# Fox attention in a two-block kernel: probabilities scaled before the value product, two heads in the column halves, head norm by channels

## The chip, the cores and the metric

One core of a Trainium2 chip. The metric is the device time in microseconds of one execution; the median of three runs is given. Engines: TensorE (PE in the profile, PEld for its weight loads), VectorE (DVE), ScalarE (ACT), GpSimd (POOL) and SyncE (SP), which issues the weight DMAs.

## The reference

Two transformer-like blocks for 512 tokens of width 1024, batch 1. The first mixes three heads' families (fox attention, an mLSTM, an HGRN2), projects by `w_out` and adds a convolved gated feed-forward; the second has a differential attention and an MLA attention. The part that is changed is the fox attention with 8 heads of 64, and the norm of its output by head:

```
s = einsum('bhqd,bhkd->bhqk', qi, k) * scale + ci[..., None] - c[:, :, None, :]
p = softmax(where(kpos <= qpos, s, -inf))
oa = einsum('bhqk,bhkd->bhqd', p, v)
ya = rms over each head's 64 channels of oa, times out_g
x = x + concatenate([ya, yb, yc]) @ w_out      # and so on
```

## The kernel before

The whole kernel is one static program. Python builds a list of stages (`order`); every engine walks the same list and issues its own share of each stage, in that order, with semaphores between the engines. So the list fixes the order of work on each engine, and what an engine does late holds back all that stands behind it in its list.

Large products are done as three fp32r products of high and low parts (L1033 to L1035: w_hi by act_hi, w_hi by act_lo, w_lo by act_hi), with activations of 512 tokens moving. Weights arrive by DMA in `w_raw` (two buffers), ScalarE rounds them to `w_hi` (stage `w_hi`), VectorE makes `w_lo` as the difference (stage `w_lo`; in the fox attention the pieces placed by "lo" are halves of 1,024 columns). Each output of 128 channels by 512 tokens is a tile; tiles take turns in two PSUM banks, `ring0` and `ring1`, in the order in which they are first opened. `open_bank` waits until the tile two places earlier has been drained. `tile_done` is one counter for all tiles, and who needs tile n waits until it is n + 1.

The fox attention (`attention("fox", ...)`, L586 and L635) runs over 32 units u, one head h of one query block qb of 128 queries, block by block, 8 heads each. k = qb + 1 key blocks are computed. Its stages are:

- `fox_s`, for two units at once, at even steps: on TensorE scores of two heads in the two row halves (L1254) plus a decay term (L1257), into bank 0 and 1; on VectorE mask and negated row maximum (L1922, with a read of the accumulator); on ScalarE exp with the row sum, into one of four buffers `Pf`.
- `fox_t`, two steps late: TensorE transposes the unit's `Pf` block by block (L1267), VectorE copies the result into `PTs` (L2270).
- `fox_v`, three steps late: TensorE multiplies with `PTs` stationary and 64 columns of the values `av` moving (L1282), into bank 4 or 5, where a query block's eight heads lie side by side, tokens on the partitions.
- After the eighth head: `ya_n` (reciprocal of the row sums, multiply L2278, square on ScalarE), `ya_v` (sum by head L2281, Ln, Exp), `ya_s` (multiply L2286), `ya` (four transposes on TensorE into a ring bank L1290, times `out_g` into `yt` L2292, high part on ScalarE), `ya_l` (low part). They stand 4, 5, 6, 7 and 8 steps behind the block's last head.

Between these, `fill_at` lists other work by step: first the last value tiles and `yb`, then for steps 5 to 37 the tiles `wo_b` 0 to 7 (L1350 to L1352: six matmuls per listed half), each drained by a VectorE add into `xT` (L2308); `w_later` puts the `w_hi` of the two `wo_a` weight chunks at steps 17 and 32, and `lo` halves of `w_lo` at 18, 20, 33 and 34. Then `wo_a` uses all of `ya`. The last entries of `fill_at` are:

```
32: [("w_later", WO_A + 1)], 33: [("lo", 2)], 34: [("wo_b", 6, 2), ("lo", 2)], 35: [("wo_b", 6, 4)],
36: wo_b(6) + [("wo_b", 7, 2), ("wo_b", 7, 4)], 37: wo_b(7), 39: [("hold_lo", False)]
```

Here ("wo_b", j, 2) and ("wo_b", j, 4) are the two halves of tile j on TensorE, and `wo_b(j)` its drain. The MLA attention of the second block (stages `mla_s`, `mla_r`, `mla_t`, `mla_v`) already scales its probabilities by rows on ScalarE after a reciprocal for two heads, and has values stationary.

Two other products in the program use column halves: `hg_win` (L1120, both halves of bank 0) and `hg_in` (L1168, two banks). The norm of q and k uses a product by the constant `blk` (ones within each 64 channels): L1187.

Of the kernel before, what the change touches and what calls it, by code (L numbers as in the profile page):

```python
# [24 lines left out]
P = 128  # L25
# [74 lines left out]
def two_blocks(nc, xt_d, w_in_d, b_in_d, w_gate_d, w_out_d, w_up_d, w_down_d, pos_d, w_in2_d, lam_d, w_uq_d, w_ukv_d,  # L100
               w_pd_d, w_pm_d, w_out2_d, g_fin_d, par_d, con_d, out_d):
    ctx = ExitStack()
    with ctx:
# [6 lines left out]
        def sem(name):  # L110
# [37 lines left out]
        fox_s_mm, fox_m, fox_e, fox_t_mm, fox_pt, fox_v_mm, fox_o_free = (  # L148
            sem(n) for n in ("fox_s_mm", "fox_m", "fox_e", "fox_t_mm", "fox_pt", "fox_v_mm", "fox_o_free"))

        ya_sq, ya_var, ya_rs, ya_n, ya_hi, ys_hi, y_lo = (sem(n) for n in ("ya_sq", "ya_var", "ya_rs", "ya_n", "ya_hi", "ys_hi", "y_lo"))
# [87 lines left out]
        on = sb("on", [P, AH, HD], F32, M + 60)  # L239
        sqA = sb("sqA", [P, AH, HD], F32, M + 62)  # L240
# [135 lines left out]
        def stage(*s):  # L376
            order.append(s)
# [208 lines left out]
        def attention(name, heads, norm, fill_at):  # L586

            n = NB * heads
            for u in range(n + 8):
# [8 lines left out]
                if name == "mla":  # L598
# [4 lines left out]
                    if u % 2 == 0 and u < n:  # L603
                        stage("mla_r", u)
                else:
# [5 lines left out]
                steps = {"ya": ("ya_n", "ya_v", "ya_s", "ya", "ya_l"), "yd": ("yd_n", "yd_s", "yd", "yd_l"), "ym": ("ym", "ym_l")}[norm]  # L611
                for late, kind in enumerate(steps, 4 if name == "fox" else 3):
# [406 lines left out]
        def _(pe):  # L1019
# [57 lines left out]
            for s in order:  # L1077
# [180 lines left out]
                elif kind == "fox_t":  # L1258
                    u = s[1]
                    qb, h = fox[u]  # L1260
                    pe.wait_ge(fox_e, u + 1)
# [7 lines left out]
                elif kind == "fox_v":  # L1269
                    u = s[1]  # L1270
                    qb, h = fox[u]
                    pe.wait_ge(fox_pt, u + 1)
# [8 lines left out]
                    for b in range(qb + 1):  # L1281
                        mm = pe.matmul(bank[4 + qb % 2][:, HD * h:HD * h + HD], PTs[u % 2][:, b * P:b * P + P],  # L1282
                                       av[:, b, HD * h:HD * h + HD], start=(b == 0), stop=(b == qb))
                    mm.then_inc(fox_v_mm, 1)
                elif kind == "ya":
                    qb = s[1]
                    out = open_bank(("ya", qb))
                    pe.wait_ge(ya_n, qb + 1)
                    for j in range(4):
                        mm = pe.transpose(out[:, j * P:j * P + P], on[:, 2 * j:2 * j + 2, :], ident)  # L1290
                    mm.then_inc(tile_done, 1)
# [264 lines left out]
        def _(act):  # L1556
# [23 lines left out]
            for s in order:  # L1580
# [134 lines left out]
                elif kind == "ya_n":  # L1715
                    qb = s[1]
                    act.wait_ge(fox_o_free, qb + 1)
                    A(sqA[:], on[:], ACT.Square).then_inc(ya_sq, 1)
                elif kind == "ya_v":
                    qb = s[1]  # L1720
                    act.wait_ge(ya_var, qb + 1)
                    A(msA, msA, ACT.Ln).then_inc(act_step, 1)
                    act.wait_ge(act_step, step())
# [186 lines left out]
        def _(dve):  # L1910
# [21 lines left out]
            for s in order:  # L1932
# [330 lines left out]
                elif kind == "fox_t":  # L2263
# [4 lines left out]
                    if u >= 2:  # L2268
                        dve.wait_ge(fox_v_mm, u - 1)
# [383 lines left out]
```

## Time and profile before

| | us |
|---|---|
| three runs | 1091.23, 1091.55, 1091.55 (median 1091.55) |
| profiled execution: time | 1091.19 |
| profiled execution: span of the core | 1089.4 |
| TensorE busy | 1076.6 (99%) |
| VectorE busy | 711.6 (65%) |
| ScalarE busy | 429.7 (39%) |
| mean granted clock of TensorE | 0.999 of full speed |

The span runs from the first to the last instruction of the profiled execution. The fox attention lies between 201 us (first scores) and 287 us (first `wo_a` matmul). An f32 matmul call is two instructions in the records (L1254: 64 records for 32 calls); a transpose and a bf16 call are one. In the timeline a matmul's own duration includes its flow through the array, so the pace is read from one start to the next, as the chain does.

### The profile page before, as it was taken

What the parts mean: (1) busy time and instruction counts of PE and PEld (TensorE: products, weight loads), DVE (VectorE), ACT (ScalarE), POOL (GpSimd) and SP (SyncE); (2) the same over time, 40 slices, a digit from 0 to 9 for tenths busy, and PEclk for the clock granted to TensorE, in tenths of its full rate; (3) what the DMA queues carried; (4) which work ended last, traced back from release to release, by engine and by line L of the source; (5) the groups of instructions that cost most, each with busy time, mean ns of one, the idle gap of its engine ahead of it and who ended that gap; (6) DMA issues with size and microseconds to landing.
All of it is one profiled execution on the core that took longest, in us unless ns stands there. A gap on an engine that the chain in (4) does not pass through costs nothing.

```text
span 1089.4 us, 13605 instructions
## 1 busy us (share of the span) xinstructions
PE 1076.6 (99%) x5395; PEld 866.6 (80%) x5395; DVE 711.6 (65%) x1142; ACT 429.7 (39%) x679; POOL 0.2 (0%) x4
## 2 busy tenths in 40 slices
PE   9999999999999999999999999999999999999998
PEld 6877877877878888888888888887776776888886
DVE  6897877867768888754478745655568445464441
ACT  6612555334352323222222234654257545323232
POOL 0000000000000000000000000000000000000000
PEclk9999999999999999999999999999999999999999
DMA  8432121131213233233422234333120321133312
GB/s 255 122 116 79 39 78 42 50 144 39 72 46 126 86 107 105 60 87 97 148 85 75 61 97 155 79 115 116 44 78 14 104 78 39 39 116 116 99 37 78
DMA packets 100239, 95.94 MB, mean 88 GB/s; under 512 B 5952, under 2 KB 91088, under 8 KB 100176
## 3 DMA queue, kind: packets, MB, share of 16 engines
q1 hardware_dynamic: 100000, 95.05, 27.8%
q8 instruction: 43, 0.70, 0.3%
q14 instruction: 20, 0.16, 0.0%
q10 hardware_dynamic: 176, 0.02, 0.0%
HBM read 92.95 MB, written 2.10 MB: 87 GB/s over the span
## 4 chain that ended last, share of the span: by engine, by line
PE 93%; DVE 3%; ACT 2%; issue 1%; DMA 0%; SPq 0%; DVEq 0%; ACTq 0%
PE ring L1033 23%; PE ring L1035 22%; PE ring L1034 22%; PE bank L1033 3%; PE bank L1035 3%; PE bank L1034 3%; PE bank L1491 1%; PE bank L1282 1%; PE bank L1254 1%; PE bank L1187 1%; PE bank L1267 1%; PE bank L1120 1%; PE bank L1460 1%; PE ring L1350 1%; PE bank L1514 1%
## 5 line engine op out<-in xcount | busy, mean ns | idle before, releaser
L1033 PE MATMUL ring<-act_hi,w_hi 128*128 128x512 f32 (+1 forms) x816 | 323.7, 397 | 0.8 <-DVE xT L2313 0.5
L1035 PE MATMUL ring<-act_hi,w_lo 128*128 128x512 f32 (+1 forms) x816 | 316.8, 388 | 0.0
L1034 PE MATMUL ring<-act_lo,w_hi 128*128 128x512 f32 (+1 forms) x816 | 316.6, 388 | 0.0
L1578 ACT ACTIVATE w_hi<-w_raw 128x2048 fp32r<-128x2048 f32 (+4 forms) x97 | 160.8, 1659 | 245.0 <-PE ring L1035 202.6
L1929 DVE TENSOR_TENSOR w_lo<-w_raw,w_hi 128x2048 fp32r<-128x2048 f32 (+5 forms) x102 | 191.4, 1879 | 3.3 <-ACT w_hi L1578 3.0
L1033 PEld LDWEIGHTS ring<-act_hi,w_hi 128*128 128x128 f32 x816 | 153.4, 188 | 37.2 <-issue 3.9
L1034 PEld LDWEIGHTS ring<-act_lo,w_hi 128*128 128x128 f32 x816 | 153.4, 188 | 31.7 <-issue 1.9
L1035 PEld LDWEIGHTS ring<-act_hi,w_lo 128*128 128x128 f32 x816 | 153.2, 188 | 31.8
L1033 PE MATMUL ring<-hidH,w_hi 128*128 128x512 f32 x176 | 68.5, 389 | 0.0
L1034 PE MATMUL ring<-hidL,w_hi 128*128 128x512 f32 x176 | 68.5, 389 | 0.0
L1035 PE MATMUL ring<-hidH,w_lo 128*128 128x512 f32 x176 | 68.5, 389 | 0.0
L2347 DVE TENSOR_TENSOR zp<-ring,rsn 128x512 f32<-128x512 f32 x44 | 30.4, 690 | 41.5 <-PE ring L1035 36.9
L1922 DVE CUSTOM_DVE_ANT_0 bank<-bank,maskb 128x128 f32<-128x128 f32 (+3 forms) x80 | 37.8, 514 | 29.1 <-PE bank L1517 14.4
L2372 DVE TENSOR_TENSOR xT<-xT,ring 128x512 f32<-128x512 f32 x16 | 11.0, 688 | 58.2 <-PE ring L1035 58.2
L1034 PEld LDWEIGHTS ring<-hidL,w_hi 128*128 128x128 f32 x176 | 33.0, 188 | 6.9
L1035 PEld LDWEIGHTS ring<-hidH,w_lo 128*128 128x128 f32 x176 | 33.0, 188 | 6.8
L1033 PEld LDWEIGHTS ring<-hidH,w_hi 128*128 128x128 f32 x176 | 33.0, 188 | 6.8
L1578 ACT ACTIVATE hidH<-hid 128x512 fp32r<-128x512 f32 x22 | 13.8, 625 | 60.3 <-DVE hid L2360 60.3
L1578 ACT ACTIVATE Pf<-bank,small 128x128 f32<-128x128 f32 (+3 forms) x32 | 16.6, 523 | 31.4 <-DVE small L1922 31.4
L1578 ACT ACTIVATE sqn<-ring 32x512 f32<-32x512 f32 x36 | 21.2, 589 | 12.5 <-PE ring L1035 12.2
L1033 PE MATMUL bank<-w_hi,mH 128*128 128x512 f32 x64 | 25.7, 402 | 0.0
L1033 PE MATMUL bank<-w_hi,act_hi 128*128 128x512 f32 x64 | 25.4, 398 | 0.0
(362 smaller groups left out, 1626.3 us busy)
## 6 DMA issues: line engine op xcount, KB each, us to landing
w_raw<-in_w_in SPq DMA_DIRECT2D x30, 1024.0 KB, 5.3
w_raw<-in_w_up SPq DMA_DIRECT2D x22, 1024.0 KB, 5.1
w_raw<-in_w_out SPq DMA_DIRECT2D x8, 1024.0 KB, 5.0
w_raw<-in_w_down SPq DMA_DIRECT2D x8, 768.0 KB, 4.6
w_raw<-in_w_down SPq DMA_DIRECT2D x8, 640.0 KB, 4.2
w_raw<-in_w_in SPq DMA_DIRECT2D x7, 512.0 KB, 5.7
xin<-in_xt SPq DMA_DIRECT2D x8, 256.0 KB, 4.1
xT<-in_xt SPq DMA_DIRECT2D x2, 1024.0 KB, 6.7
```

The costliest lines, as they stand in the source:

```text
L1033: pe.matmul(out, ah, bh, start=(first and n == 0), stop=False)
L1034: pe.matmul(out, ah, bl, start=False, stop=False)
L1035: mm = pe.matmul(out, al, bh, start=False, stop=(last and n == len(pairs) - 1))
L1120: mm = pe.matmul(v3(bank[0][64 * p:64 * p + 64, :], LC)[:, :, first:], con[:, row:row + 64], v3(Ab[n % 6][:, p, :], LC)[:, :, first:], sta ...
L1187: pe.matmul(nrm_bank(n)[:], cc("blk"), scr[n % 2][:], start=True, stop=True).then_inc(nrm_mm, 1)
L1254: pe.matmul(bank[e][:, 0:n], qT[r, h // 2, qb * P:qb * P + P], kT[r, h // 2, 0:n], start=True, stop=False)
L1267: mm = pe.transpose(bank[2 + u % 2][:, b * P:b * P + P], Pf[u % 4][:, b * P:b * P + P], ident)
L1578: return act.activation(out, src, func, **more)
L1922: return dve.tensor_tensor_reduce(scores[:, 0:n], scores[:, 0:n], maskb[:, T - n:T], -1.0, 3.0e38, ALU.add, ALU.min, least)
L1929: return TT(dst, full, hi.bitcast(F32), ALU.subtract)
L2347: TT(z[:, 2:T + 2], at_ring(s)[:], rsn[:], ALU.mult).then_inc(bank_free(s), 1)
L2372: TT(xT[:, j, :], xT[:, j, :], at_ring(s)[:], ALU.add).then_inc(bank_free(s), 1)
```

## The change

The probabilities are divided by their row sums before they are transposed: a new stage `fox_r`, once for two units, takes a reciprocal on VectorE and scales two rows of `Pf` on ScalarE. The value product has 64 columns of values stationary and `PTs` moving, two heads in the two column halves of the array, so that the result has channels on the partitions and needs no transposes; `fox_v` is now one stage for two units, at even steps, four steps late, and stands ahead of `fox_t`. The head norm works by channels: square of the bank on ScalarE (`ya_q`), one product by `blk` on TensorE into a ring bank (`ya`), Ln and Exp over 128x512 on ScalarE, then on VectorE times `out_g` and times the bank (`ya_s`), and the low part (`ya_l`). These stand 3, 4, 5 and 6 steps behind the block's last head; the ring tile of `ya` is opened at steps 11, 19, 27 and 35 where it was 14, 22, 30 and 38. Besides `rsY` takes the place of `on` in memory.

```diff
--- before.py
+++ after.py
@@ -145,10 +145,10 @@
 
         yb_var, yb_rs, yb_n = (sem(n) for n in ("yb_var", "yb_rs", "yb_n"))
 
-        fox_s_mm, fox_m, fox_e, fox_t_mm, fox_pt, fox_v_mm, fox_o_free = (
-            sem(n) for n in ("fox_s_mm", "fox_m", "fox_e", "fox_t_mm", "fox_pt", "fox_v_mm", "fox_o_free"))
-
-        ya_sq, ya_var, ya_rs, ya_n, ya_hi, ys_hi, y_lo = (sem(n) for n in ("ya_sq", "ya_var", "ya_rs", "ya_n", "ya_hi", "ys_hi", "y_lo"))
+        fox_s_mm, fox_m, fox_e, fox_r, fox_n, fox_t_mm, fox_pt, fox_v_mm, fox_o_free = (
+            sem(n) for n in ("fox_s_mm", "fox_m", "fox_e", "fox_r", "fox_n", "fox_t_mm", "fox_pt", "fox_v_mm", "fox_o_free"))
+
+        ya_sq, ya_rs, ya_hi, ys_hi, y_lo = (sem(n) for n in ("ya_sq", "ya_rs", "ya_hi", "ys_hi", "y_lo"))
 
         n_sq, n_acc, n_mm, n_rs, col_mm, n_hi, n_lo = (sem(n) for n in ("n_sq", "n_acc", "n_mm", "n_rs", "col_mm", "n_hi", "n_lo"))
 
@@ -236,8 +236,8 @@
         sqB = sb("sqB", [P, NB, BH, HD], F32, M + 18)
         Pf = [sb(f"Pf{i}", [P, T], F32, M + (52, 54, 66, 68)[i]) for i in range(4)]
         PTs = [sb(f"PTs{i}", [P, T], F32, M + 56 + 2 * i) for i in range(2)]
-        on = sb("on", [P, AH, HD], F32, M + 60)
-        sqA = sb("sqA", [P, AH, HD], F32, M + 62)
+        rsY = sb("rsY", [P, T], F32, M + 60)
+        sqA = sb("sqA", [P, T], F32, M + 62)
         yt = sb("yt", [P, 4, P], F32, M + 64)
 
         xT = sb("xT", [P, KD, T], F32, M)
@@ -602,14 +602,21 @@
                             stage(name + kind, u - late + 1)
                     if u % 2 == 0 and u < n:
                         stage("mla_r", u)
+                elif name == "fox":
+                    if u % 2 == 0 and 4 <= u < n + 4:
+                        stage("fox_v", u - 4)
+                    if 2 <= u < n + 2:
+                        stage("fox_t", u - 2)
+                    if u % 2 == 1 and u < n:
+                        stage("fox_r", u - 1)
                 else:
                     if 2 <= u < n + 2:
                         stage(name + "_t", u - 2)
                     if 3 <= u < n + 3:
                         stage(name + "_v", u - 3)
 
-                steps = {"ya": ("ya_n", "ya_v", "ya_s", "ya", "ya_l"), "yd": ("yd_n", "yd_s", "yd", "yd_l"), "ym": ("ym", "ym_l")}[norm]
-                for late, kind in enumerate(steps, 4 if name == "fox" else 3):
+                steps = {"ya": ("ya_q", "ya", "ya_s", "ya_l"), "yd": ("yd_n", "yd_s", "yd", "yd_l"), "ym": ("ym", "ym_l")}[norm]
+                for late, kind in enumerate(steps, 3):
                     qb = (u - late) // heads
                     if (u - late) % heads == heads - 1 and 0 <= qb < NB:
                         if kind == norm and norm != "ym":
@@ -1258,7 +1265,7 @@
                 elif kind == "fox_t":
                     u = s[1]
                     qb, h = fox[u]
-                    pe.wait_ge(fox_e, u + 1)
+                    pe.wait_ge(fox_n, u + 1)
                     if u == 1:
                         pe.wait_ge(ml_o_s, 4)
                     if u >= 2:
@@ -1269,7 +1276,7 @@
                 elif kind == "fox_v":
                     u = s[1]
                     qb, h = fox[u]
-                    pe.wait_ge(fox_pt, u + 1)
+                    pe.wait_ge(fox_pt, u + 2)
                     if u == 0:
                         pe.wait_ge(nrm_rs, 10)
                     if qb % 2 == 0 and h % 4 == 0:
@@ -1279,16 +1286,16 @@
                         if qb >= 2:
                             pe.wait_ge(fox_o_free, qb - 1)
                     for b in range(qb + 1):
-                        mm = pe.matmul(bank[4 + qb % 2][:, HD * h:HD * h + HD], PTs[u % 2][:, b * P:b * P + P],
-                                       av[:, b, HD * h:HD * h + HD], start=(b == 0), stop=(b == qb))
+                        for e in range(2):
+                            mm = pe.matmul(bank[4 + qb % 2][64 * e:64 * e + 64, P * (h // 2):P * (h // 2) + P],
+                                           av[:, b, HD * (h + e):HD * (h + e) + HD], PTs[e][:, b * P:b * P + P],
+                                           start=(b == 0), stop=(b == qb))
                     mm.then_inc(fox_v_mm, 1)
                 elif kind == "ya":
                     qb = s[1]
                     out = open_bank(("ya", qb))
-                    pe.wait_ge(ya_n, qb + 1)
-                    for j in range(4):
-                        mm = pe.transpose(out[:, j * P:j * P + P], on[:, 2 * j:2 * j + 2, :], ident)
-                    mm.then_inc(tile_done, 1)
+                    pe.wait_ge(ya_sq, qb + 1)
+                    pe.matmul(out[:], cc("blk"), sqA[:], start=True, stop=True).then_inc(tile_done, 1)
                 elif kind == "begin" and s[1] == "a_v":
                     tokens(s[1:3], f"a_v{s[2] // 2}", s[2] % 2, act, begun=s[3], until=s[4])
                 elif kind == "begin" and s[1] in ("b_qk", "a_q", "a_k"):
@@ -1712,19 +1719,28 @@
                         act.wait_ge(fox_t_mm, u - 3)
                     A(Pf[u % 4][:, 0:n], bank[u % 2][:, 0:n], ACT.Exp, scale=-1.0, bias=nmx[:, u % 4:u % 4 + 1],
                       accum_out=rsum[:, 8 * (qb % 2) + h:8 * (qb % 2) + h + 1]).then_inc(fox_e, 1)
-                elif kind == "ya_n":
+                elif kind == "fox_r":
+
+                    act.wait_ge(fox_r, s[1] // 2 + 1)
+                    for u in (s[1], s[1] + 1):
+                        qb, h = fox[u]
+                        row = Pf[u % 4][:, 0:(qb + 1) * P]
+                        A(row, row, ACT.Identity, scale=recA[:, h:h + 1]).then_inc(fox_n, 1)
+                elif kind == "ya_q":
+                    qb = s[1]
+                    act.wait_ge(fox_v_mm, AH // 2 * (qb + 1))
+                    A(sqA[:], bank[4 + qb % 2][:], ACT.Square).then_inc(ya_sq, 1)
+                elif kind == "ya":
+                    qb = s[1]
+                    act.wait_ge(tile_done, upto(s))
+                    if qb >= 1:
+                        act.wait_ge(fox_o_free, qb)
+                    A(rsY[:], at_ring(s)[:], ACT.Ln, bias=cc("eps"), scale=1.0 / HD).then_inc(bank_free(s), 1)
+                    act.wait_ge(bank_free(s), drains(s))
+                    A(rsY[:], rsY[:], ACT.Exp, scale=-0.5).then_inc(ya_rs, 1)
+                elif kind == "ya_s":
                     qb = s[1]
                     act.wait_ge(fox_o_free, qb + 1)
-                    A(sqA[:], on[:], ACT.Square).then_inc(ya_sq, 1)
-                elif kind == "ya_v":
-                    qb = s[1]
-                    act.wait_ge(ya_var, qb + 1)
-                    A(msA, msA, ACT.Ln).then_inc(act_step, 1)
-                    act.wait_ge(act_step, step())
-                    A(rsA, msA, ACT.Exp, scale=-0.5).then_inc(ya_rs, 1)
-                elif kind == "ya":
-                    qb = s[1]
-                    act.wait_ge(bank_free(s), drains(s))
                     A(hH[:, 0:4, qb * P:qb * P + P], yt[:], ACT.Identity).then_inc(ya_hi, 1)
                 elif kind == "y_split":
                     i = s[1]
@@ -2266,30 +2282,25 @@
                     n = (qb + 1) * P
                     dve.wait_ge(fox_t_mm, u + 1)
                     if u >= 2:
-                        dve.wait_ge(fox_v_mm, u - 1)
+                        dve.wait_ge(fox_v_mm, u // 2)
                     CP(PTs[u % 2][:, 0:n], bank[2 + u % 2][:, 0:n]).then_inc(fox_pt, 1)
-                elif kind == "ya_n":
+                elif kind == "fox_r":
+
+                    u = s[1]
+                    qb, h = fox[u]
+                    dve.wait_ge(fox_e, u + 2)
+                    if u >= AH:
+                        dve.wait_ge(fox_n, u - AH + 2)
+                    at = 8 * (qb % 2) + h
+                    dve.reciprocal(recA[:, h:h + 2], rsum[:, at:at + 2]).then_inc(fox_r, 1)
+                elif kind == "ya_s":
                     qb = s[1]
-                    dve.wait_ge(fox_v_mm, AH * (qb + 1))
-                    dve.reciprocal(recA, rsum[:, 8 * (qb % 2):8 * (qb % 2) + 8]).then_inc(dve_step, 1)
-                    dve.wait_ge(dve_step, step())
-                    if qb >= 1:
-                        dve.wait_ge(tile_done, upto(("ya", qb - 1)))
-                    TT(on[:], v3(bank[4 + qb % 2][:], HD), wide(recA, HD), ALU.mult).then_inc(fox_o_free, 1)
-                elif kind == "ya_v":
-                    dve.wait_ge(ya_sq, s[1] + 1)
-                    dve.tensor_reduce(msA, sqA[:], AX.X, ALU.add).then_inc(dve_step, 1)
-                    dve.wait_ge(dve_step, step())
-                    TS(msA, msA, 1.0 / HD, EPS, ALU.mult, ALU.add).then_inc(ya_var, 1)
-                elif kind == "ya_s":
-                    dve.wait_ge(ya_rs, s[1] + 1)
-                    TT(on[:], on[:], wide(rsA, HD), ALU.mult).then_inc(ya_n, 1)
-                elif kind == "ya":
-                    qb = s[1]
-                    dve.wait_ge(tile_done, upto(s))
+                    dve.wait_ge(ya_rs, qb + 1)
+                    TT(v3(rsY[:], P), v3(rsY[:], P), wide(pc("g_out", 0, 4), P), ALU.mult).then_inc(dve_step, 1)
+                    dve.wait_ge(dve_step, step())
                     if qb >= 1:
                         dve.wait_ge(ya_hi, qb)
-                    TT(yt[:], v3(at_ring(s)[:], P), wide(pc("g_out", 0, 4), P), ALU.mult).then_inc(bank_free(s), 1)
+                    TT(yt[:], v3(bank[4 + qb % 2][:], P), v3(rsY[:], P), ALU.mult).then_inc(fox_o_free, 1)
                 elif kind == "ya_l":
                     qb = s[1]
                     dve.wait_ge(ya_hi, qb + 1)
```

## Rows read from the trace of the kernel before

**Rows 1.** The page: TensorE's busy time, and the chain that ended last, by engine.
```profile
PE 1076.6 (99%) x5395; PEld 866.6 (80%) x5395; DVE 711.6 (65%) x1142; ACT 429.7 (39%) x679; POOL 0.2 (0%) x4
...
PE 93%; DVE 3%; ACT 2%; issue 1%; DMA 0%; SPq 0%; DVEq 0%; ACTq 0%
```

**Rows 2.** Busy time (x instructions) in 259 to 281 us: PE, PEld, DVE, ACT, POOL; clock, DMA.
```profile
259.00:281.00 22.00, 21.83 (x160) 17.54 (x157) 17.94 (x38) 9.27 (x21) 0.00 (x0) 1.00 0.01 1
```

**Rows 3.** Chain that ended last, 195 to 295 us: start us, us, what, x instructions.
```profile
200.16 0.87 PE bank L1187 x2
...
244.63 0.84 PE bank L1254 x4
...
266.25 0.23 PE ring L1350
...
266.94 0.44 PE bank L1267 x4
...
267.38 0.84 PE bank L1282 x8
...
268.22 1.06 PE bank L1254 x4
...
275.34 0.44 PE ring L1290 x4
```

**Rows 4.** The same chain at the two products in column halves, L1120 and L1168.
```profile
85.49 3.28 PE bank L1120 x16
...
112.24 1.90 PE bank L1168 x32
```

**Rows 5.** Timeline at L1168, weight loads: start us, us, engine, line, what.
```profile
112.17 1.73 PEld L1168 LDWEIGHTS bank<-Dm,ci 128*64 128x64 f32 x32
```

**Rows 6.** Timeline of the MLA attention: value product, reciprocal, scaling of two probability rows.
```profile
916.03 1.60 PE L1491 MATMUL bank<-PT,mv 128*128 128x128 f32 x12
...
918.94 0.16 DVE L2510 RECIPROCAL small<-small 128x2 f32<-128x2 f32 x1
...
919.13 1.34 ACT L1578 ACTIVATE Pm<-Pm,small 128x512 f32<-128x512 f32 x2 [0.65 <-DVE small L2510]
```

**Rows 7.** Timeline of one pair of heads of query block 3 on VectorE and ScalarE.
```profile
264.33 0.70 DVE L1922 CUSTOM_DVE_ANT_0 bank<-bank,maskb 128x512 f32<-128x512 f32 x1 [1.33 <-PE bank L1257]
...
265.59 0.68 DVE L2270 COPY PTs<-bank 128x512 f32<-128x512 f32 x1
...
265.80 0.68 ACT L1578 ACTIVATE Pf<-bank,small 128x512 f32<-128x512 f32 x1
...
266.37 0.20 ACT L1578 ACTIVATION_READ_ACCUMULATOR Pf<-bank,small 128x1 f32 x1
```

**Rows 8.** Timeline of query block 2: splits, copy, exp, multiply, square.
```profile
244.00 1.91 ACT L1578 ACTIVATE w_hi<-w_raw 128x2048 fp32r<-128x2048 f32 x1
...
246.67 0.55 DVE L2270 COPY PTs<-bank 128x384 f32<-128x384 f32 x1
...
246.90 0.57 ACT L1578 ACTIVATE Pf<-bank,small 128x384 f32<-128x384 f32 x1
...
247.14 1.22 DVE L1929 TENSOR_TENSOR w_lo<-w_raw,w_hi 128x1024 fp32r<-128x1024 f32 x1
...
249.02 0.69 DVE L2278 TENSOR_TENSOR on<-bank,small 128x512 f32<-128x512 f32 x1
...
249.74 0.63 ACT L1578 ACTIVATE sqA<-on 128x512 f32<-128x512 f32 x1 [2.18 <-DVE on L2278]
```

**Rows 9.** Timeline, TensorE's idle time in brackets (us, released by) where it waits.
```profile
214.37 0.66 PE L1234 MATMUL ring<-con,onB 128*128 128x128 f32 x4 [0.35 <-DVE av L2041]
...
242.36 0.50 PE L1350 MATMUL ring<-yH,w_hi 128*128 128x512 f32 x1 [0.51 <-DVE xT L2308]
...
271.53 1.10 PE L1282 MATMUL bank<-av,PTs 128*128 128x64 f32 x8 [0.17 <-DVE PTs L2270]
...
287.01 0.45 PE L1033 MATMUL ring<-act_hi,w_hi 128*128 128x384 f32 x1 [0.34 <-DVE xT L2308]
```

## The prediction

> **What bounds the kernel now.** I read the page first: the engines' shares, then the chain of work that ended last. TensorE is busy for 99% of the span and carries 93% of that chain [rows 1], so a microsecond of TensorE's time is a microsecond of the kernel, and so is every microsecond for which it is made to wait. Then the busy times by stretch, for the part where the fox attention runs (from 201 to 287 us). In the last query block TensorE is busy for 21.8 of 22 us, but VectorE for 17.9 and ScalarE for only 9.3 [rows 2]. The reader should see two things there: TensorE has no slack to hide anything in, and VectorE, which is not the bound, has 4 us left in 22. Last I read the timeline of this part, unit by unit, since the change re-orders it: what counts is how far each transpose and each value product on TensorE lies behind the copy, reciprocal or exp that feeds it.
>
> **TensorE's own work.** A unit is one head in one query block; block qb has k = qb+1 key blocks. The value product is 80 calls, each of two instructions. Eight take 0.84 us, 0.105 each [rows 3]: 64 moving columns cost as much as the load of 128 stationary columns. All 160 cost 16.8 us. After, 64 columns are stationary, 128 move, and two heads go to the two column halves. The trace has this form: L1168, 32 instructions in 1.90 us, 0.059 each [rows 4], into two different banks; L1120 writes both halves of the same bank, as the new code does, and needs 3.28 us for 16 instructions of 416 to 512 columns (7,424 in all), 0.44 ns a column, 0.057 for 128. So the halves overlap, in one bank too. Weight loads of L1168 follow each other every 0.0515 us ((1.73-0.14)/31) [rows 5]; what is left of its 1.90 us is the price of entering and leaving the column mode, 0.19 to 0.25 us. The new code enters it 16 times, between the row-tiled scores and the full-array transposes. I take 4k x 0.0535 + 0.19 for a pair of heads: 0.40, 0.62, 0.83, 1.05 us for k = 1 to 4, four times each, 11.6 us in all (bounds: 160 x 0.059 = 9.4, and 12.2 with 0.0515 and 0.25). Saved: 5.2 us (4.6 to 7.4). The head norm exchanges four transposes (0.44 us) for one f32 product by the constant blk over 512 columns; L1187 is that product: 0.87 us for its two instructions [rows 3]. Four times +0.43 is +1.7. TensorE's work alone: -3.5 us (bounds -5.7 and -2.9).
>
> The row on weight loads can be weighed against a rule. The Trainium skill, TensorE: Matmul & The Clock Gate, "Measured speedup vs the span model" and what stands ahead of it, has weight loads overlap running matmuls only when their row groups differ. Column halves share their row group, so by that rule the loads of the new product would stand bare and this term would be a loss. L1168 has one row group and a load every 0.0515 us while 128-column matmuls run, so the trace speaks against it here.
>
> **The other engines.** Reciprocals are now per pair (0.16 us [rows 6]), 16 of them. VectorE loses, per query block, a reciprocal, three multiplies of 512 columns and a reduction (about 3.1 us) and gains four reciprocals and two multiplies (2.1 us). ScalarE gains the scaling of every probability row: two rows of 512 take 1.34 us and two of 384 about 1.12 by the same row's rate [rows 6], some 16 us in the stage, plus Ln and Exp over 512 columns in place of two tiny ones. Both engines have room on average. The order is what costs.
>
> **The new waits.** I walked the stage list of the new attention loop pair by pair, with these durations: scores 0.84 (qb 2) and 1.06 (qb 3) [rows 3] and some 0.2 for the decay term, transposes 0.33 and 0.44 per unit [rows 3], plus 0.15 where they follow a tiled product; a wo_b fill of six matmuls 6 x 0.23 = 1.4; two masked minima 1.26 (qb 3: from the first one's start to the copy behind the second), exp 0.68 each plus 0.2 for the sum, PTs copy 0.68 [rows 7]; for qb 2 copy 0.55, exp 0.58; whi split 1.91, half a wlo split 1.22, a 512-column multiply 0.69, the square 0.63 [rows 8]. A hand-over costs 0.02 to 0.1. In most pairs TensorE stays ahead-fed by 0.1 to 0.4 us. These places do not:
>
> 1. *Start.* The reciprocal of units 0 and 1 lies ahead of yb_norm on VectorE, in a stretch where TensorE already waits for VectorE (second yb, 0.35 idle [rows 9]): +0.2, and v0, which stood ahead of that wait, now comes behind it: +0.2. Sum 0.4.
> 2. *ya of block 0* now stands at step 11, one step behind its square, and the transpose of unit 12 needs a scaling that ScalarE does behind Ln, Exp and the yt split: 0.4.
> 3. *ya of block 1*, step 19. The square stands on ScalarE behind exp 18 and 19, and these behind the whi split put in at step 17, and that behind the scaling of units 16 and 17, which waits for the copy of unit 15. From the end of transpose 15: copy 0.45, reciprocal 0.2, scalings 1.12, split 1.91, exps 1.35, square 0.65, hand-over 0.1: 5.8 us. TensorE has scores 1.0, product 0.62, transpose 0.48, fill 1.4, transpose 0.33: 3.8. Stall 1.95.
> 4. *Value product of 18 and 19*, step 22. VectorE from the end of scores 20/21: until transpose 18 is there 1.3, copy 0.55, two multiplies of ya_s 1.38, half a wlo split 1.22, copy 19 0.55, hand-over 0.1: 5.1. TensorE meanwhile 4.05. Stall 1.05.
> 5. *The end of block 3*, where TensorE has no fills: value product of 26 waits for the copy of 27. From transpose 26: copy 0.68, ya_s 1.38, xT add 0.68, copy 0.68, hand-over 0.1: 3.5 against transpose 0.44 + scores 1.28. Stall 1.8. Then VectorE is the bound: reciprocal, ya_l, two minima, two copies, 3.5 us, against 2.1 us on TensorE: 1.4. The last product needs two copies (1.4 us) behind one transpose (0.44): 1.0. Sum 4.2.
> 6. *wo_b 7*. Tiles take the two ring banks in turn. Before, wo_b 7 follows wo_b 6; ya of block 3 comes last. Now ya is opened at step 35, between them, so wo_b 7 needs the bank of wo_b 6, which VectorE drains at step 36 behind ya_s, and that behind Ln and Exp. Moreover tile_done is one counter: Ln waits for a count that is only reached once wo_b 6 too is finished. So from wo_b 6's last matmul: 0.69 + 0.63 + 0.69 + 0.69 + 0.68 + hand-overs = 3.5 us, and nothing on TensorE beside it.
>
> Sum 11.5 us. Waits that go: 0.5 at 242.36 (xT drain behind ya_l, which now comes two steps sooner), 0.2 at 271.53, 0.3 at 287.01 [rows 9]: 1.0. So -3.5 + 11.5 - 1.0 = +7.0. The profiled execution took 1091.19 us (span 1089.4), 0.36 below the median of 1091.55; I forecast a span near 1096.4 and a time of 1098.4. Behind 287 us TensorE is again the bound, so nothing is given back.
>
> **Rivals.**
> *TensorE stays the bound* (ends on the other side). If VectorE and ScalarE run ahead enough, only -3.5 - 1.0 is left: 1087. For it: the averages of [rows 2]. Against: it needs the stalls of items 3 to 6, each worked out from its own chain, to sum to under 4.5 us; item 6 alone is 3.5. 10%.
> *Half the stalls.* Consecutive VectorE operations overlap by some 0.05 us, and an early lead absorbs part of items 3 to 5; with 3 to 4 us of 7.2 left there: 1094.5. 20%. *About level*: item 6 does not stand (the drain is earlier than I read) and the rest is halved, 1091.5. 10%.
> *The column halves don't overlap.* By L1491 (128x128 stationary, 128 moving, 12 in 1.60 us, 0.13 each [rows 6]) the product would cost 160 x 0.13 = 21 us, 4 more than now, 9 more than I take, of which the stalls hide a third: 1104. The weight-load rule of the Trainium skill's page above would lead there. Against it stand both rows 4. 5%.
>
> **Numbers.** My forecast, all six items, has 55%, with its own range 1096 to 1100.5. Differences under 0.2% (2.2 us) are about what a measurement of this kernel can't tell from no change. Faster: 10%. Same: the level case and a tail of the half-stall case, 13%. Slower: 77%. The range goes from 1091 to 1101.5: it leaves out the faster case, the 1104 case and some of the forecast's own tail.
>
> **What would show it.** Right: L1282's successor at 0.05 to 0.065 us an instruction; TensorE idle before ya at steps 19 (released by ScalarE's square), before value products (released by PTs copies) in the last 14 us of the attention, and, the largest single one, about 3.5 us before wo_b 7's first matmul, released by the xT add; the stretch from the scores of units 28 and 29 (268.22 [rows 3]) to the first wo_a matmul (287.01 [rows 9]) grows from 18.8 us by some 5. Wrong: no idle time before wo_b 7; the product at 0.1 us or more; or gaps of under 0.3 us where I put 1 to 2, which would mean that the engines run ahead of my walk.

## The result, and the profile after

The changed kernel takes 1098.24 us (median of 6 runs, 1097.97 to 1098.57), the kernel before 1091.55 on the same chip (1091.23 to 1091.67): a ratio of 1.0063, 95% interval 1.0053 to 1.0073, slower by 6.7 us. The forecast was 1098.4. The profiled execution has a span of 1096.4 us against 1089.4.

The page after, at the places of [rows 1]: TensorE's busy time and the chain that ended last, by engine.

```profile
PE 1074.5 (98%) x5387; PEld 856.8 (78%) x5387; DVE 707.9 (65%) x1142; ACT 448.4 (41%) x711; POOL 0.2 (0%) x4
...
PE 91%; DVE 4%; ACT 2%; issue 2%; DMA 1%; DVEq 0%; ACTq 0%
```

TensorE is busy for 2.1 us less, and yet the span is 7.0 us longer: the engine stands still. Where it does is in its waits between 200 and 300 us (engine and line, releaser: us in total, times, longest):

```profile
PE bank L1290 <- DVE PTs L2286: 3.8, 4, 1.1
PE ring L1357 <- DVE xT L2319: 3.5, 1, 3.5
PE ring L1298 <- ACT sqA L1585: 1.5, 1, 1.5
PE ring L1241 <- DVE av L2057: 0.6, 1, 0.6
PE bank L1261 <- ACT Pf L1585: 0.6, 1, 0.6
```

These are 10.0 us, against 1.4 us in [rows 9] (1.6 by the same view of the kernel before, which also has one of 0.2 us behind the first wo_a matmul). L1290 is the value product (L1282 before), L1298 the product ya, L1357 to L1359 the wo_b matmuls, L1261 the scores. Where each wait lies, in TensorE's timeline of the changed kernel (the wait in brackets, with its releaser):

```profile
248.54 1.10 PE L1298 MATMUL ring<-sqA,con 128*128 128x512 f32 x2 [1.45 <-ACT sqA L1585]
...
255.51 0.88 PE L1290 MATMUL bank<-PTs,av 128*64 128x128 f32 x12 [0.86 <-DVE PTs L2286]
...
268.13 1.13 PE L1261 MATMUL bank<-kT,qT 64*128 64x512 f32 x4
...
272.13 1.13 PE L1261 MATMUL bank<-kT,qT 64*128 64x512 f32 x4 [0.61 <-ACT Pf L1585]
...
274.39 1.10 PE L1290 MATMUL bank<-PTs,av 128*64 128x128 f32 x16 [0.91 <-DVE PTs L2286]
...
277.63 1.09 PE L1290 MATMUL bank<-PTs,av 128*64 128x128 f32 x16 [1.13 <-DVE PTs L2286]
...
280.70 1.09 PE L1290 MATMUL bank<-PTs,av 128*64 128x128 f32 x16 [0.94 <-DVE PTs L2286]
...
289.11 0.80 PE L1357 MATMUL ring<-yH,w_hi 128*128 128x512 f32 x1 [3.48 <-DVE xT L2319]
289.70 0.63 PE L1358 MATMUL ring<-yL,w_hi 128*128 128x512 f32 x1
290.12 0.63 PE L1359 MATMUL ring<-yH,w_lo 128*128 128x512 f32 x1
...
293.31 0.33 PE L1040 MATMUL ring<-act_hi,w_hi 128*128 128x384 f32 x1
```

The reader should take three marks from it. The scores of units 28 and 29 start at 268.13 us; before they started at 268.15 in the same view (268.22 in the chain, [rows 3]): up to here saving and stalls cancel. The first wo_a matmul starts at 293.31 instead of 287.01 [rows 9], 6.3 us later: nearly the whole loss falls in the last 25 us of the stage. And the matmuls behind the 3.48 us wait start 0.43 us apart where the same ones start 0.23 apart otherwise.

The windows say the same (PE, PEld, DVE, ACT and POOL busy; then clock and DMA). The first row is the window of [rows 2]; TensorE's 21.83 us became 18.40, ScalarE's 9.27 became 16.26. The second holds the slow matmuls.

```profile
259.00:281.00 22.00, 18.40 (x154) 11.93 (x152) 15.47 (x38) 16.26 (x31) 0.00 (x0) 1.00 0.02 7
...
283.00:300.00 17.00, 13.52 (x69) 11.59 (x68) 4.59 (x8) 4.16 (x5) 0.00 (x0) 0.90 0.20 62
```

The new product in the chain, at the places of L1282 in [rows 3] and with the form of [rows 4]:

```profile
226.88 0.37 PE bank L1290 x4
...
233.81 0.59 PE bank L1290 x8
...
250.65 0.81 PE bank L1290 x12
...
269.47 1.02 PE bank L1290 x16
```

Each four instructions more cost 0.22 us, 0.054 an instruction, and 0.15 us come on top per visit.

### The profile page after: what moved, and what is told of

It is laid out like the page before. It is cut to its first block, busy times and chain, and to the rows that moved or that the text cites. A ratio compares the mean times of both kernels' runs of the same rounds, so it can differ in the third digit from the quotient of the medians.

```text
span 1096.4 us, 13639 instructions
## 1 busy us (share of the span) xinstructions
PE 1074.5 (98%) x5387; PEld 856.8 (78%) x5387; DVE 707.9 (65%) x1142; ACT 448.4 (41%) x711; POOL 0.2 (0%) x4
## 4 chain that ended last, share of the span: by engine, by line
PE 91%; DVE 4%; ACT 2%; issue 2%; DMA 1%; DVEq 0%; ACTq 0%
PE ring L1040 22%; PE ring L1042 22%; PE ring L1041 22%; PE bank L1040 3%; PE bank L1042 3%; PE bank L1041 3%; PE bank L1498 1%; DVE w_lo L1945 1%; PE bank L1290 1%; PE bank L1194 1%; PE bank L1127 1%; PE bank L1467 1%; PE bank L1261 1%; PE bank L1521 1%; PE bank L1274 1%
## 5 line engine op out<-in xcount | busy, mean ns | idle before, releaser
L1042 PE MATMUL bank<-w_hi,mL 128*128 128x512 f32 x64 | 25.0, 391 | 0.0
```

The source lines that it names most:

```text
L1042: mm = pe.matmul(out, al, bh, start=False, stop=(last and n == len(pairs) - 1))
```

## The experiments

Each is timed beside the kernel before, whose median was 1090.97 to 1091.38 us there. "After" is the changed kernel. The expectations count the stretch from the first exp of the fox attention (203.7 us before, 203.6 after) to the first drain of wo_a (292.8 and 299.0): 89.1 us before, 95.4 after. It leaves out what other parts of the kernel add. "Local" below is this stretch, read from one profiled execution, so it can differ by 1 us or so from what the medians say.

**1. The order of the ring tiles.** In the changed kernel ya of block 3, and what follows it, is put off by two steps, so that it comes behind wo_b 7, as it did before the change.

```
+ if name == "fox" and kind != "ya_q" and u >= 34:
+     late += 2
```

> The changed kernel with the norm tile ya of query block 3 opened at step 37 instead of 35 (its later stages two steps later too), so that wo_b 7 follows wo_b 6 in the ring and its bank comes from ya of block 2. Theory (the ring order makes TensorE wait 3.5 us, and the idle time costs another 1.2 us because six matmuls after it run at 0.43 us instead of 0.23): the idle time before wo_b 7 goes, no slow matmuls, time 1098.2 - 4.7 + up to 0.7 for a wait that may appear at the first wo_a tile: 1093.5 to 1094.2. Rival (the wait is VectorE's and ScalarE's chain itself and moves to wo_a): the stall re-appears before the second part of wo_a 0, time 1097 to 1098.

Measured: 1093.92 us (1093.55 to 1094.42), 1.0025 [1.0016, 1.0035]; local 91.0, 4.4 less than after. In the timeline of this kernel wo_b 7 follows wo_b 6 without a wait at 0.23 us, and ya comes last:

```profile
284.39 0.39 PE L1361 MATMUL ring<-yH,w_lo 128*128 128x512 f32 x1
284.62 0.39 PE L1359 MATMUL ring<-yH,w_hi 128*128 128x512 f32 x1
...
287.34 1.03 PE L1300 MATMUL ring<-sqA,con 128*128 128x512 f32 x2
```

What follows: the place of one tile in the ring is worth 4.3 us of the 6.7: the forecast's 3.5 us wait and the slow matmuls behind it, less a few tenths (a wait of 0.2 us has come in wo_a).

**2. Is the slow pace the idle time's doing?** Twelve matmuls into a bank that nothing reads are put ahead of wo_b 7. They are additional work; nothing of the computation changes.

```
+ if (name, j, k0) == ("wo_b", 7, 0):
+     wh, wl = weights("wo_b1")
+     for _ in range(12):
+         pe.matmul(bank[0][:], wh[:, 0, 0:P], yH[:, 0, :], start=True, stop=True)
```

> The changed kernel with 12 additional full-size matmuls into a bank that nobody reads, on TensorE just ahead of the wait before wo_b 7; output unchanged. Theory (the clock fell because TensorE idled): the wait still ends at the same moment, the extra work fills 2.8 of the 3.5 us, and the six matmuls behind it run at 0.23 us: time 1098.2 - 1.2 = 1097.0. Rival (the slow matmuls come from something else, such as operand traffic on the shared memory): they stay at 0.43 us and the time stays 1098.2.

Measured: 1096.28 us (1095.95 to 1096.46), 1.0045 [1.0033, 1.0058]; local 94.1, 1.3 less than after, 2.0 less on the device. The timeline of this kernel:

```profile
285.63 2.90 PE L1353 MATMUL bank<-yH,w_hi 128*128 128x512 f32 x12
289.29 0.50 PE L1361 MATMUL ring<-yH,w_hi 128*128 128x512 f32 x1 [0.75 <-DVE xT L2323]
289.63 0.40 PE L1362 MATMUL ring<-yL,w_hi 128*128 128x512 f32 x1
```

wo_b 7 starts no sooner, 289.29 against 289.11, but at 0.23 us a matmul, and the granted clock of 283 to 300 us is 1.00 instead of 0.90. The slow pace came from the idle time, and cost 1.3 us. (The other 0.7 us are the wait for sacc at 684.78 us of the changed kernel, below; this kernel's trace doesn't have it.)

**3. The tail of block 3.** ya_s and ya_l of block 2 are taken off steps 28 and 29 and put at step 33, out of VectorE's way.

```
+ if name == "fox" and kind in ("ya_s", "ya_l") and u in (28, 29):
+     continue
+ if name == "fox" and u == 33 and kind in ("ya_s", "ya_l"):
+     stage(kind, 2)
```

> The changed kernel with ya_s and ya_l of query block 2 moved from steps 28 and 29 to step 33, behind the last copy, so that VectorE has 2.1 us less between the copies of units 26 and 31. Theory (VectorE's order makes TensorE wait for units 28 to 31): the waits of 0.6 (scores of 30) and 0.9 us (value product of 26) go, the 1.1 before the product of 28 shrinks to under 0.5, the last one (0.9) stays; time 1098.2 - 2.1 = 1096.1. Rival (ScalarE's scalings are what is late): the waits stay within 0.3 us and the time within 0.5 us of 1098.2.

Measured: 1098.48 us (1097.24 to 1098.88), 1.0065 [1.0051, 1.0079], level with the changed kernel where I expected 1096.1; local 94.6, only 0.8 less, and that in the fastest of its five executions (1097.24). One of the four waits of the tail is gone, the one at the product of 26, and the one at the product of 28 is 0.94 instead of 1.13 us. The others stand in this kernel's timeline as in the changed one:

```profile
272.45 1.13 PE L1265 MATMUL bank<-kT,qT 64*128 64x512 f32 x4 [0.61 <-ACT Pf L1589]
...
273.73 1.09 PE L1294 MATMUL bank<-PTs,av 128*64 128x128 f32 x16
...
276.79 1.09 PE L1294 MATMUL bank<-PTs,av 128*64 128x128 f32 x16 [0.94 <-DVE PTs L2290]
...
279.85 1.09 PE L1294 MATMUL bank<-PTs,av 128*64 128x128 f32 x16 [0.94 <-DVE PTs L2290]
```

The starts 276.79 and 279.85 are 3.06 us apart, as 277.63 and 280.70 are in the changed kernel (3.07): transposes, two copies one behind the other, product. ya_s in VectorE's queue was not what held them, so my expectation was wrong. The loop of dependent steps was.

**4. The weight split of block 2.** The 1.9 us split that ScalarE makes at step 17 is moved to step 19, and the wlo halves to 21 and 23.

```
- ... 17: [("w_later", WO_A)], 18: [("wo_b", 3, 4), ("lo", 2)], 19: wo_b(3), 20: [("wo_b", 4, 2), ("lo", 2)], ... 23: wo_b(4),
+ ... 18: [("wo_b", 3, 4)], 19: wo_b(3) + [("w_later", WO_A)], 20: [("wo_b", 4, 2)], 21: [("lo", 2)], ... 23: wo_b(4) + [("lo", 2)],
```

> The changed kernel with the weight split w_hi of the first wo_a chunk moved from step 17 to 19 and its two w_lo halves from 18 and 20 to 21 and 23, all behind the scaling or reciprocal of their step. Theory (the 1.9 us split on ScalarE ahead of exp 18 and 19 delays the square for ya of block 1, and half a w_lo delays the copy of unit 19): TensorE's waits of 1.45 us before ya and 0.9 us before the value product of 18 go: time 1098.2 - 2.3 = 1095.9. Rival (Ln and Exp of ya or the scalings hold it up in any case): the waits stay or come back two pairs later, time within 0.7 us of 1098.2.

Measured: 1098.70 us (1098.35 to 1099.27), 1.0069 [1.0057, 1.0082], where I expected 1095.9; local 94.6, 0.8 less. The waits of items 3 and 4 are gone, 2.3 us, and two others have come, 1.15 and 0.22 us, at the scores of 22 and 24 (timeline of this kernel, ScalarE and TensorE):

```profile
250.60 1.90 ACT L1585 ACTIVATE w_hi<-w_raw 128x2048 fp32r<-128x2048 f32 x1
252.40 0.56 ACT L1585 ACTIVATE Pf<-bank,small 128x384 f32<-128x384 f32 x1
...
253.67 0.92 PE L1261 MATMUL bank<-kT,qT 64*128 64x384 f32 x4 [1.15 <-ACT Pf L1585]
```

The split now stands ahead of the exps of 20 and 21, and the next scores need the banks that these read. Item 3's mechanism is shown, the split in front of a square or of an exp; at neither of the two places tried does ScalarE have a gap of 1.9 us without TensorE paying for it. The 0.8 us don't reach the device's time: this trace has a wait of 0.98 us at 976.32 us, far behind the attention, that the changed kernel's doesn't have. Where it comes from isn't settled.

**5. Do the column halves overlap?** The two loops of the product are exchanged: all of one head, then all of the other.

```
- for b in range(qb + 1):
-     for e in range(2):
+ for e in range(2):
+     for b in range(qb + 1):
```

> The changed kernel with the value product issued head by head (all key blocks of one column half, then all of the other) instead of the two halves in turn; same work, same results. Theory (a pair costs 4k x 0.0535 us only because instructions in different halves overlap): a block-3 pair takes 16 x 0.107 = 1.7 us instead of 1.0, all 16 pairs 7 us more, of which the waits behind them hide about 2: time 1102 to 1105. Rival (halves overlap whatever the order, or don't overlap in either): pairs stay at 1.0 us and the time at 1098.2.

Measured: 1101.98 us (1101.27 to 1102.68), 1.0099 [1.0086, 1.0113], 3.7 us over the changed kernel; local 99.6, 4.2 more. The chain of this kernel has the same 12 and 16 instructions at 1.07 and 1.51 us, where the changed kernel's takes 0.81 and 1.02; 4 and 8 instructions take 0.37 and 0.59 in both:

```profile
233.54 0.59 PE bank L1290 x8
...
250.38 1.07 PE bank L1290 x12
...
270.27 1.51 PE bank L1290 x16
```

With 16 instructions, the halves in turn cost 0.064 us each, entry included, one head behind the other 0.094. So the overlap exists, and with three and four key blocks (6 and 8 instructions of one half in a row) it is bound to the order; with one and two key blocks the order makes no difference. In all the order adds 4 x (0.26 + 0.49) = 3.0 us of product, not the 7 that I expected. Another 1.4 us of the 4.2 are the clock: behind the same wait of 3.48 us the slow matmuls last here until 297.6 us, 5.3 us long instead of 2.5 (granted clock of 283 to 300 us 0.80, 0.90 in the changed kernel). TensorE's waits are 0.4 us shorter. Even one head behind the other the product takes 4 x (0.37 + 0.59 + 1.07 + 1.51) = 14.2 us, less than the 8 x (0.17 + 0.39 + 0.62 + 0.84) = 16.2 of the kernel before by its chain: of the 5.0 us that the new form saves, 3.0 hang on issuing the halves in turn.

**6. Experiments 1, 3 and 4 together.**

> The changed kernel with the three re-orderings of e1_ring, e3_tail and e4_split together. Theory (the change does save 3.5 us on TensorE and loses it only to order): 1098.2 - 4.7 - 2.1 - 2.3 = 1089.1, within 1088.3 to 1090.5, so 1 to 3 us below the kernel before the change. Rival (the saving on TensorE is not there, or waits re-appear elsewhere): 1091.5 or more.

Measured: 1091.91 us (1091.61 to 1092.23), 1.0007 [0.9998, 1.0016]; local 88.8, 0.3 under the kernel before. I expected 1089.1, from the gains that I had expected of the three; what they measured one by one (local 4.4, 0.8 and 0.8) adds up to 6.0, and together they give 6.6. TensorE's waits between 200 and 300 us:

```profile
PE bank L1267 <- ACT Pf L1591: 2.0, 3, 1.2
PE bank L1296 <- DVE PTs L2292: 1.9, 2, 0.9
PE ring L1247 <- DVE av L2063: 0.6, 1, 0.6
```

With the two of 0.2 us that follow them in this view they sum to 4.9 us against 1.6 before by the same view, 3.3 more; that the stretch is still 0.3 shorter leaves 3.6 us less of TensorE's own work, the term that I had at 3.5.

**7. Fills for the tail.** wo_b 6 is moved to steps 29 to 31 and wo_b 7 to 31 to 34 (ya of block 3 then follows both), in the changed kernel otherwise as it is; `hold_hi` holds back the weight split that follows wo_b 7. **8.** The same with the moves of 3 and 4. The core of the edit:

```
- ... 34: [("wo_b", 6, 2), ("lo", 2)], 35: [("wo_b", 6, 4)], 36: wo_b(6) + [("wo_b", 7, 2), ("wo_b", 7, 4)], 37: wo_b(7), ...
+ ... 29: [("wo_b", 6, 2)], 30: [("wo_b", 6, 4)], 31: wo_b(6) + [("wo_b", 7, 2)], 32: [("wo_b", 7, 4), ("w_later", WO_A + 1)],
+ 33: [("lo", 2), ("hold_hi", True)], 34: wo_b(7) + [("lo", 2)], 37: [("hold_hi", False)], ...
```

> The changed kernel with the matmuls of wo_b 6 and 7 moved from steps 34 to 36 to steps 29 to 32, between the units of the last query block, where TensorE had no other work and waited; their drains move with them, and the weight split that follows wo_b 7 is held back to step 37. Nothing else changes. Theory (in block 3 TensorE is now faster than the path scores, minimum, exp, scaling, transpose, copy, so only other work can fill): the waits of 0.6, 0.9, 1.1 and 0.9 us and the 3.5 us before wo_b 7 with the slow matmuls behind it (1.2) go, 8.2 us together; a wait of 0.7 to 1.2 us for the square appears before ya of block 3: time 1098.2 - 7.3 = 1090.9. Rival (VectorE is the bound there, whatever fills): only the 4.7 us of e1_ring go: 1093.5 or more.

> e7_fills together with the re-orderings of e3_tail and e4_split. Theory: the local gains of those two (0.8 and 0.7 us from the first exp to the first wo_a drain) come on top only in part, since the tail's waits are gone already: 0.5 to 1 us under e7_fills, 1090.2. Rival (they were worth something only while the tail waited): the same as e7_fills within 0.4 us.

Measured: 1094.54 us (1093.61 to 1095.64), 1.0029 [1.0018, 1.0041], and 1095.00 us (1092.65 to 1095.80), 1.0030 [1.0019, 1.0041]. Against the changed kernel they gain 3.7 and 3.2 us, half or less of what I expected of them (7.3 and 8.0). In the timeline of experiment 7 a fill now waits itself, for the ring bank of wo_b 5, whose drain stands behind ya_s of block 2, and slow matmuls follow:

```profile
273.83 0.50 PE L1357 MATMUL ring<-yH,w_hi 128*128 128x512 f32 x1 [2.27 <-DVE xT L2319]
...
274.92 0.63 PE L1357 MATMUL ring<-yH,w_hi 128*128 128x512 f32 x1
275.34 0.63 PE L1358 MATMUL ring<-yL,w_hi 128*128 128x512 f32 x1
```

In experiment 8 no wait of this stage is longer than 1.47 us, and the slow pace comes all the same. Waits of 0.78, 1.47 and 0.91 us end at 283.78, 286.35 and 288.36 us, and behind them the 384-column wo_a matmuls start 0.32 us apart until 291.81, 0.17 to 0.18 from 292.10 on:

```profile
286.35 1.10 PE L1302 MATMUL ring<-sqA,con 128*128 128x512 f32 x2 [1.47 <-ACT sqA L1589]
...
288.36 0.46 PE L1044 MATMUL ring<-act_hi,w_hi 128*128 128x384 f32 x1 [0.91 <-DVE xT L2323]
...
289.25 0.52 PE L1044 MATMUL ring<-act_hi,w_hi 128*128 128x384 f32 x1
289.57 0.52 PE L1045 MATMUL ring<-act_lo,w_hi 128*128 128x384 f32 x1
```

Of its seven executions the fastest (1092.65 us) had a mean granted clock of 0.999, the slowest (1095.80) 0.996: how long the clock is low differs from one execution to the next, and with it the time.

**9. The same fills in the kernel before.** It has no overlap of halves and no new norm.

> The kernel before the change, with wo_b 6 and 7 moved to steps 29 to 32 in the same way. Its norm of block 3 (reciprocal, multiply, square, sum, Ln, Exp, multiply, then transposes on TensorE) has nothing left to hide behind. Theory (the old norm needs this work as cover, the new one does not): TensorE waits some 4 us before the transposes of ya of block 3, time 1091.3 + 4 - 0.2 = 1095. Rival (the re-ordering helps either form): 1091 or less.

Measured: 1100.65 us (1099.48 to 1101.12), 1.0083 [1.0070, 1.0097]. The kernel before is made slower by the same move, by more than I expected: a fill waits 1.61 us for its ring bank, and in its timeline the transposes of ya, now the last thing of the stage with nothing beside them, wait 5.5 us, and the wo_a matmuls behind them run 0.32 us apart instead of 0.17 to 0.18 as in the changed kernel (293.31, 293.48, 293.66).

```profile
294.00 1.09 PE L1290 MATMUL ring<-con,on 128*128 128x128 f32 x4 [5.48 <-DVE on L2286]
...
295.53 0.52 PE L1035 MATMUL ring<-act_hi,w_lo 128*128 128x384 f32 x1
295.85 0.52 PE L1033 MATMUL ring<-act_hi,w_hi 128*128 128x384 f32 x1
```

So the order before was no accident of the old norm: wo_b 6 and 7 at the end cover it.

**10. and 11. A best version.** Fills of wo_b 6 at steps 30, 32 and 33, wo_b 7 whole at 34, the tail of experiment 3; the 1.9 us split at step 4 (10) or at step 19 (11).

```
  ... 30: [("wo_b", 6, 2)], 32: [("wo_b", 6, 4), ("w_later", WO_A + 1)], 33: wo_b(6) + [("hold_hi", True)],
  34: [("wo_b", 7, 2), ("wo_b", 7, 4), ("lo", 2)] + wo_b(7), 37: [("hold_hi", False), ("lo", 2)], ...
```

> The changed kernel with: ya_s and ya_l of block 2 at step 33; the first wo_a chunk's w_hi split at step 4, where ScalarE idles, with its w_lo halves at 21 and 23; wo_b 6 on TensorE at steps 30 and 32 with its drain at 33, wo_b 7 whole at step 34 with its drain there, ahead of ya of block 3; the weight split behind it held to step 37. The wo_b 5 drain now comes before wo_b 6 is opened (in e7_fills it came behind and cost 2.3 us and slow matmuls). Theory (all of the change's loss is order): of e6_all's waits the 1.2 us before the scores of unit 22 and most of the 2.5 us in block 3 go: 1091.9 - 3.2 = 1088.7, and 1087.5 to 1090.3. Rival (each re-ordering opens a new wait of its own size): 1091.5 or more, as e7_fills and e8_best did.

> e10_best with the first wo_a chunk's w_hi split back at step 19, as in e4_split and e6_all: at step 4 ScalarE waited 4.8 us for the weights' DMA, TensorE 3.9 us for a scaling behind it, and matmuls ran slowly after that. Theory: the 3.9 us and some 3 us of slow matmuls go, 1.2 us before the scores of unit 22 come back; the last part of the attention keeps its shape of e10_best, 0.5 us better than e6_all: 1091.2 to 1091.6, level with the kernel before. Rival (the tail of e10_best was good only because the head was late): 1092.5 or more.

Measured: 1095.51 us (1095.34 to 1097.12), 1.0044 [1.0030, 1.0058], and 1091.18 us (1090.58 to 1091.78) against 1090.99, 1.0001 [0.9992, 1.0010]; the second is what I expected, the first is 6.8 us over. In experiment 10 the timeline shows that the raw weights weren't there yet at step 4: the split waits for its DMA, the scalings of a pair wait behind it, and TensorE for these; the wo_b matmuls behind start 0.43 us apart (229.20, 229.62).

```profile
226.25 1.91 ACT L1589 ACTIVATE w_hi<-w_raw 128x2048 fp32r<-128x2048 f32 x1 [4.83 <-DMA w_raw<-in_w_out]
...
228.50 0.47 PE L1278 MATMUL bank<-con,Pf 128*128 128x128 f32 x1 [3.87 <-ACT Pf L1589]
```

Experiment 11 is the best version of the change that I found, and it is level with the kernel before: no version here beats it.

## Why the prediction was right, and where its steps were not

*TensorE's work (-3.5).* Right in sum, and near in its terms. The product costs 4 x (0.37 + 0.59 + 0.81 + 1.02) = 11.2 us, where the sum had 11.6 (and 16.2 before, where it had 16.8); the pace of 0.0535 holds, and the price of the mode is 0.15 a visit instead of 0.19. ya is one pair of instructions, 0.86 us in the chain at two of its places and 0.96 and 1.10 at the others, where the sum had 0.87. Two sums over the run agree: the stretch to the first wo_a matmul is 6.3 us longer, with 8.6 us more waiting (10.0 less 1.4) and 1.4 us of slow clock (the 12 matmuls of wo_b 7 take 293.31 - 289.11 = 4.2 us instead of 12 x 0.23 = 2.8), so the work is 3.7 us less; experiment 6 gives 3.6. The rival in which the halves don't overlap is refuted. So is, for this form, the rule that the prediction had weighed: the Trainium skill, TensorE: Matmul & The Clock Gate, Part 3, "The mechanism", lists that weight loads overlap running matmuls only when the row groups differ (the text above that list also names loads into a background weight buffer; no run here can tell which is at work). The trace disagrees with the list: sixteen loads and matmuls of one row group take 1.02 us, and one such load by itself is 0.137 us long.

*Item 1 (0.4).* 0.6 at the second yb against 0.35 before: +0.25.

*Item 2 (0.4).* Did not appear: TensorE's timeline has no wait there.

*Item 3 (1.95).* 1.45 us, at the place and by the releaser forecast; it goes when the split is moved (experiment 4).

*Item 4 (1.05).* 0.86 us, likewise gone with experiment 4. That experiment moves ScalarE's split and VectorE's two wlo halves together, so which of them makes this wait isn't shown apart.

*Item 5 (4.2).* The size is near, 0.61 + 0.91 + 1.13 + 0.94 = 3.6 us, the account of it is only half right. I had put 1.8 us down to ya_s and the xT add ahead of the copy of 27. That wait is 0.91. Taking ya_s and ya_l away (experiment 3; the xT add stayed) took away it and 0.2 us of the next. The rest is latency, and one part of it I hadn't named: the scores of 30 wait 0.61 us for the exp of 29, since scores, two minima and two exps take longer than product and transposes now do on TensorE. The faster product shortened the work that covered this loop.

*Item 6 (3.5).* 3.48 us; the chain after runs as it was walked. Its pieces, with no TensorE among them:

```profile
285.66 0.70 ACT rsY L1585
286.38 0.64 ACT rsY L1585
...
287.04 0.70 DVE rsY L2299
...
287.77 0.69 DVE yt L2303
288.46 0.60 DVE xT L2319
```

*Waits that go (1.0).* The 0.5 us at 242.36 and the 0.3 at the first wo_a matmul are gone; the product's 0.17 became one of the 0.9.

*What the sum did not have.* The slow matmuls behind item 6's wait, 1.3 to 1.4 us by the timeline and by experiment 2, and 0.7 us far behind the attention, where TensorE waits at 684.78 us for VectorE's sacc; all the versions but experiment 2 have it too, with 0.4 to 0.7 us; the kernel before and experiment 9 don't. In the trace it hangs on a weight split that ScalarE begins 7.0 us later than before (680.22 against 673.24), when its DMA has landed, while the work around it is 6.2 us later. Why that transfer is late isn't settled; no experiment was made on it.

So the direction and the large stalls came as forecast, but that the total is right to 0.2 us is luck: two kinds of error offset each other. New stalls of 11.5 us were forecast and 10.0 are there in TensorE's row by the waits of after, of which 0.35 at the second yb stood there before; the clock and the late transfer, 2.0 us together, were not foreseen. That also shows in time: I expected the last stretch, from the scores of 28 and 29 to wo_a, to grow by 5 us and what lies ahead of it by the rest; it grew from 18.9 to 25.2 (by the timelines), 1.4 of that the clock, and ahead of it nothing was lost.

The level rival falls with item 6, which stands in full. The half-stall rival had item 6 in it too; it left 3 to 4 us of the 7.2 in items 3 to 5, and 1.45 + 0.86 + 3.6 = 5.9 are there. The time of 1087 that the rival with TensorE as the only bound gave is reached by none of the versions. Even with item 6 undone the change gives nothing back: experiments 6 and 11 still have 4 to 5 us of waits. The saving of 3.6 us goes into the latency of a pair (scores, minima, exps, reciprocal, scalings, transposes, copies, product), which grew by the reciprocal and the scalings while the work beside it shrank.

## What to carry to other kernels

Here the bounding engine was 99% busy, and still a saving on it was only real as far as the dependent steps on the others still fitted beside what was left. So walk the loop once with the new durations, and the order of every buffer ring and every counter that several tiles share, before counting the saving. A tile opened between two others in a ring of two makes the third wait for the whole life of the first's drain, 3.5 us here. Moving a long piece on a helper engine moved the wait in experiments 4 and 10 instead of removing it: look for a gap of its length in that engine's row, at a time when its input has landed.

## What the hardware showed that was not expected

- TensorE's clock fell in the midst of a kernel that keeps it 98% busy. Behind idle times of 3.48, 2.27, 3.87 and 5.48 us (after, experiments 7, 10 and 9) 512-column matmuls start 0.43 us apart and 384-column ones 0.32 apart, which is the 1.2 GHz level; otherwise 0.23 and 0.17, the 2.4 GHz level. The slow ones lasted from 289.70 to 292.17 us in the changed kernel and from about 294.7 to 298.4 in experiment 9. Behind the idle times of 1.45 and 1.13 us in the changed kernel the pace stayed; with its own 3.48 us filled down to 0.75 (experiment 2) the clock stayed at 1.00. But one long wait isn't needed: in experiment 8 the slow pace came behind 0.78, 1.47 and 0.91 us, which end within 4.6 us. And the same 3.48 us were followed by 2.5 us of slow matmuls in the changed kernel and by 5.3 us in experiment 5.
- The two column halves work beside each other within one bank and one row group in full only if they are issued in turn: 1.02 us for 16 instructions, 1.51 with one head behind the other (0.81 and 1.07 for 12). For 4 and 8 instructions the order costs nothing, 0.37 and 0.59 us either way.
